# Block 1's first output product: six of its eight units as seven block products each

## The reference

```python
S, D, H = 512, 2048, 8
# first_block: y_mlstm (S, D) and y_sgu (S, D) are both gated activations
x = x + concat([y_mlstm, y_sgu], axis=-1) @ w_out      # w_out (2 D, D), fp32
x = rms_norm(x, final_norm_w)
# second_block: 16 meta tokens are put ahead of x, a layer norm, then two hybrid layers
# (convolution, windowed attention, a gated recurrence), each ending in a product and a layer norm
```

## Time and profile before

| | us |
|---|---|
| median of 3 runs | 3236.39 (3235.48 to 3239.59) |
| the profiled execution's own time | 3235.69 |
| its span, first to last instruction | 3234.2 |
| PE busy | 3149.7 (97%) |
| DVE busy | 2160.9 (67%) |
| ACT busy | 1516.4 (47%) |
| POOL busy | 334.1 (10%) |

### The profile page before, as it was taken

The page is one execution under the profiler, slowest core; times in us unless marked ns, Lnnn a source line. Parts: engine busy times, 40 slices in busy tenths (PEclk is TensorE's granted clock), DMA queues, the critical chain, the costliest instruction groups (busy, mean ns, idle before and its releaser), DMA issues.

```text
span 3234.2 us, 59399 instructions
## 1 busy us (share of the span) xinstructions
PE 3149.7 (97%) x22670; PEld 2932.9 (91%) x22670; DVE 2160.9 (67%) x2930; ACT 1516.4 (47%) x2444; POOL 334.1 (10%) x343
## 2 busy tenths in 40 slices
PE   8999999999999999999979999999997999999998
PEld 7899999999999998788869999999997888888898
DVE  6677888888888888226785655657458565556535
ACT  5345555555555555222254555556226355545521
POOL 1000000000000000000000430440000134314000
PEclk9999999999999999999989999999998999999999
DMA  6344434433434435523334222222333422222522
GB/s 206 92 105 110 107 99 106 124 103 105 110 98 109 108 100 187 182 85 101 102 104 133 67 79 74 60 79 89 137 104 111 138 79 78 72 73 65 171 92 92
DMA packets 449806, 342.51 MB, mean 106 GB/s; under 512 B 20889, under 2 KB 439641, under 8 KB 446449
## 3 DMA queue, kind: packets, MB, share of 16 engines
q1 hardware_dynamic: 431808, 296.28, 31.3%
q0 software_dynamic: 8304, 26.92, 2.3%
q10 hardware_dynamic: 9552, 17.37, 1.6%
HBM read 315.04 MB, written 25.46 MB: 105 GB/s over the span
## 4 chain that ended last, share of the span: by engine, by line
PE 86%; DVE 7%; ACT 3%; DVEq 2%; issue 2%; DMA 1%; ACTq 0%; SPq 0%; POOL 0%
PE ps L696 14%; PE ps L697 14%; PE ps L698 14%; PE ps L866 9%; PE ps L869 9%; PE ps L868 8%; PE ps L1095 2%; PE ps L1256 1%; PE ps L1254 1%; PE ps L1258 1%; PE ps L936 1%; PE ps L702 1%; PE ps L703 1%; PE ps L704 1%; DVE w_low L1947 1%
## 5 line engine op out<-in xcount | busy, mean ns | idle before, releaser
L696 PE MATMUL ps<-x_high,w_high 128*128 128x264 f32 (+3 forms) x3264 | 1068.2, 327 | 52.0 <-DVE w_low L1947 23.0
L697 PE MATMUL ps<-x_low,w_high 128*128 128x264 f32 (+3 forms) x3264 | 1037.6, 318 | 0.0
L698 PE MATMUL ps<-x_high,w_low 128*128 128x264 f32 (+3 forms) x3264 | 1034.9, 317 | 0.0
L696 PEld LDWEIGHTS ps<-x_high,w_high 128*128 128x128 f32 x3264 | 619.1, 190 | 102.9 <-issue 55.8
L1947 DVE TENSOR_TENSOR w_low<-w_raw,w_high 128x1024 fp32r<-128x1024 f32 x332 | 405.6, 1229 | 441.4 <-ACT w_high L1296 416.8
L697 PEld LDWEIGHTS ps<-x_low,w_high 128*128 128x128 f32 x3264 | 619.4, 190 | 44.3 <-issue 3.3
L698 PEld LDWEIGHTS ps<-x_high,w_low 128*128 128x128 f32 x3264 | 617.8, 189 | 41.3
L1296 ACT ACTIVATE w_high<-w_raw 128x1024 fp32r<-128x1024 f32 x332 | 350.2, 1057 | 319.0 <-PE ps L698 247.3
L866 PE MATMUL ps<-x_high,w_high_blocks 128*128 128x256 f32 x1600 | 456.6, 285 | 0.0
L869 PE MATMUL ps<-x_high,w_low_blocks 128*128 128x256 f32 x1600 | 449.4, 281 | 0.0
L868 PE MATMUL ps<-x_low,w_high_blocks 128*128 128x256 f32 x1600 | 449.4, 281 | 0.0
(11 more groups left out here) (471 smaller groups left out, 4817.7 us busy)
## 6 DMA issues: line engine op xcount, KB each, us to landing
w_raw_blocks<-in_w_in SPq DMA_DIRECT2D x200, 512.0 KB, 5.0
w_raw<-in_w_in SPq DMA_DIRECT2D x384, 256.0 KB, 3.2
w_raw<-in_w_out SPq DMA_DIRECT2D x272, 256.0 KB, 3.0
residual<-residual_stream ACTq DMA_DIRECT2D x8, 1056.0 KB, 10.2
residual_stream<-y_layer ACTq DMA_DIRECT2D x2, 2176.0 KB, 9.7
x_natural<-in_x SPq DMA_DIRECT2D x4, 1024.0 KB, 9.3
x_feature_major<-x_stage POOLq DMA_DIRECT2D x4, 1024.0 KB, 6.7
y_sgu_feature_major<-z_silu_g POOLq DMA_DIRECT2D x8, 512.0 KB, 5.1
```

The costliest lines, as they stand in the source:

```text
L696: pe.matmul(dst, wh[:, j, kt, wc], xh[:, k, tok], start=first, stop=False)
L697: pe.matmul(dst, wh[:, j, kt, wc], xl[:, k, tok], start=False, stop=False)
L698: return pe.matmul(dst, wl[:, j, kt, wc], xh[:, k, tok], start=False, stop=last)
```

## The change

Product G keeps two plain units (`PLAIN_G = 2`) and does the other six as block units. What is new around them:

- The four sums of activation blocks are formed by DVE from the staged `y_sgu` (`yst`), before the low weights of the second plain unit, and split by ACT and DVE during that unit; S4's sum is split last, since it goes into the part of x_high and x_low that the second unit still reads.
- The six block units have buffers of their own for the weight sum and the partial results, and use PSUM banks 4 to 6.
- The upper half of `acc` is loaded after three of the sums are split (they lie in its place); the wait for it moves to the fourth block unit (`add_blocks`, k == 8).
- `y_mlstm` is now staged and split around the last block unit, in the manner in which `y_sgu` is before product G.
- PE waits for `c11`, `c12` and `c21` before the meta transposes.
- Loops over product G are written out, and the parameter rows of the second block are loaded later.
- The scratch of POOL's transfers (`dynamic_dma_scratch_size`) is set to 4096 bytes.

```diff
+PLAIN_G = 2
+U_OUT_M = U_OUT_G + PLAIN_G
+SLOT_G = (1, 2, 3, 0, 1, 2, 3)
+def banks_out(e):
+    return tuple(4 + b for b in banks_sgu(e % 3))
...
 # SyncE
-            for d in range(1, 3):
+            for d in range(1, PLAIN_G):
                 load(U_OUT_G + d, cols(w_out, 256 * d, row=KT))
-            sp.wait_ge(x_ready, 2 * KT)
+            for e in range(8 - PLAIN_G):
+                c = 256 * (PLAIN_G + e)
+                load_blocks(S_END + e, c, c + P, 0 if e else PG, w_out, KT)
+            for j in range(4):
+                sp.wait_ge(lo_ready, done(S_GEND - 1, B_S4 if j == 3 else B_S3))
...
             sp.wait_ge(y_st, 32 * H)
             for j in range(4):
+                sp.wait_ge(piece_used, done(S_GEND - 1, B_S2 + j // 2))
                 sp.dma_start(yst[:, 4 * j:4 * j + 4, :], y_md[:, 4 * j:4 * j + 4, :]).then_inc(part_in[j], 16)
 # GpSimd
+            pool.wait_ge(s_low, 14)
             pool.dma_start(acc[:, 8:16, :], x_t[:, 8:16, :]).then_inc(acc_in, 16)
-            pool.wait_ge(y_st, 32 * H)
+            pool.wait_ge(s_low, 16)
             pool.dma_start(mnat[:], a["meta_tokens_2"]).then_inc(meta_in, 16)
...
             pool.wait_ge(acc_in, 48)
+            pool.wait_ge(piece_used, done(S_GEND - 1, B_S3))
             parameters(0)
 # TensorE
-            with pe.Fori(0, 8) as d:
+            for d in range(PLAIN_G):
                 unit(U_OUT_G + d, KT)
-            pe.wait_ge(c21, S_END + 1)
+            pe.wait_ge(ym_done, H + 1)
+            for e in range(8 - PLAIN_G):
+                unit_blocks(S_END + e, banks_out(e), SLOT_G)
+            passed_blocks = NBLOCK_G
+            for n in (c11, c12, c21):
+                pe.wait_ge(n, S_GEND + 1)
 # ScalarE: the last block unit, s + 1 == S_GEND
+                for j in range(3):
                     high(U_OUT_M, j)
+                act.wait_ge(piece_used, done(s, B_S4))
+                for j in range(2):
                     act.wait_ge(part_in[j], 48)
                     fill_piece(j, yst, slice(NM, L))
+                high(U_OUT_M, 3)
+                act.wait_ge(piece_used, done(s, B_A22))
+                act.wait_ge(tmp_used, 2 + 2 * PLAIN_G + 2 * e)
+                corner(s, banks, tmp[:, 0, SH:S])
+                for j in range(2, 4):
+                    act.wait_ge(part_in[j], 48)
+                    fill_piece(j, yst, slice(NM, L))
 # VectorE: ahead of the second plain unit
+            for n, a_, b_, op in ((B_S3, yst[:, K1, T2], yst[:, K1, T1], ALU.subtract), (B_S2, sf_g[B_S3], yst[:, K2, T2], ALU.subtract),
+                                  (B_S1, yst[:, K1, T2], yst[:, K2, T2], ALU.subtract), (B_S4, sf_g[B_S2], yst[:, K2, T1], ALU.add)):
+                dve.drain()
+                if n == B_S4:
+                    dve.wait_ge(y_st, 32 * H)
+                for q in range(2):
+                    ins = dve.tensor_tensor(half(sf_g[n], q), half(a_, q), half(b_, q), op)
+                ins.then_inc(s_sum, 1)
+            dve.wait_ge(acc_in, 32)
...
-    nc = bacc.Bacc("TRN2", target_bir_lowering=False, num_devices=1)
+    nc = bacc.Bacc("TRN2", target_bir_lowering=False, num_devices=1, dynamic_dma_scratch_size=4096)
```

More of the change, by code:

```diff
@@ L71 @@
 U_OUT_G = U_SGU + 3 * PLAIN
-U_OUT_M = U_OUT_G + 8
+PLAIN_G = 2
+U_OUT_M = U_OUT_G + PLAIN_G
 U_LAYER = U_OUT_M + 9
@@ L1613, in norm_mean @@
+            with act.Fori(0, 6) as d:
+                for m in range(2):
+                    act.wait_ge(tmp_used, 16 + 2 * d + m + 1)
+                    take(U_OUT_M + d, m, tmp[:, m, :], ps[:, m, :])
+                    if m == 0:
+                        for j in range(4):
+                            high(U_OUT_M + d + 1, j)
             def norm_mean(n, q):
@@ L2128, in sum_parts, with split_low @@
                 ins.then_inc(s_sum, 1)
-            def split_low(n, src, first):
+            def split_low(n, src, first, blocks=sblk):
                 for q in range(2):
@@ L2491, in _, with add, add_blocks @@
             dve.memset(small[:, 59:60], LN_EPS * EPS).then_inc(tmp_used, 2)
+            def add(U, k):
+                for m in range(2):
+                    dve.wait_ge(evac, 2 * U + m + 1)
+                    dve.tensor_tensor(acc[:, k + m, :], acc[:, k + m, :], tmp[:, m, :], ALU.add).then_inc(tmp_used, 1)
+            def add_blocks(s, k):
+                dve.wait_ge(c21, s + 2)
+                dve.drain()
+                if k == 8:
+                    dve.wait_ge(acc_in, 48)
+                for m in range(2):
+                    dve.tensor_tensor(acc[:, k + m, :], acc[:, k + m, :], tmp[:, m, :], ALU.add).then_inc(tmp_used, 1)
+                dve.drain()
@@ new lines, in _ @@
+            dve.wait_ge(acc_in, 32)
+            for d in range(PLAIN_G):
+                U = U_OUT_G + d
+                if d + 1 < PLAIN_G:
+                    lows(U + 1)
+                    add(U, 2 * d)
+                else:
+                    for i, n in enumerate((B_S3, B_S1, B_S2)):
+                        split_low(n, sf_g[n], 8 + 2 * i, sblk_g)
+                    sum_1(S_END)
+                    sum_3(S_END)
+                    low_block(S_END, B_A11, SLOT_G[B_A11])
+                    sum_2(S_END)
+                    low_block(S_END, B_A12, SLOT_G[B_A12])
+                    low_block(S_END, B_S2, SLOT_G[B_S2])
+                    add(U, 2 * d)
+                    low_block(S_END, B_S1, SLOT_G[B_S1])
+                    sum_4(S_END)
+                    split_low(B_S4, sf_g[B_S4], 14, sblk_g)
@@ new lines, in _ @@
+            for e in range(8 - PLAIN_G):
+                s = S_END + e
+                banks = banks_out(e)
+                low_block(s, B_S3, SLOT_G[B_S3])
+                if e:
+                    add_blocks(s - 1, 2 * PLAIN_G + 2 * e - 2)
+                out_11(s, banks, tmp[:, 0, 0:SH])
+                low_block(s, B_S4, SLOT_G[B_S4])
+                low_block(s, B_A22, SLOT_G[B_A22])
+                if s + 1 < S_GEND:
+                    sum_1(s + 1)
+                    out_22(s, banks, tmp[:, 1, SH:S])
+                    sum_3(s + 1)
+                    low_block(s + 1, B_A11, SLOT_G[B_A11])
+                    sum_2(s + 1)
+                    out_12(s, banks, tmp[:, 1, 0:SH])
+                    low_block(s + 1, B_A12, SLOT_G[B_A12])
+                    low_block(s + 1, B_S2, SLOT_G[B_S2])
+                    low_block(s + 1, B_S1, SLOT_G[B_S1])
+                    sum_4(s + 1)
+                    continue
+                passed_blocks = NBLOCK_G
+                low(U_OUT_M, 0)
+                out_22(s, banks, tmp[:, 1, SH:S])
+                low(U_OUT_M, 1)
+                out_12(s, banks, tmp[:, 1, 0:SH])
+                for j in range(4):
+                    fill_piece(j, yst, slice(NM, L), 2 * KT)
+                    if j == 1:
+                        low(U_OUT_M, 2)
+                        low(U_OUT_M, 3)
+                add_blocks(s, 14)
```

193 lines of the change are left out of this document (112 added, 81 removed).

## The result

The changed kernel takes 3243.38 us (median; 3241.16 to 3247.45), the kernel before in the same comparison 3237.51 us. The ratio is 1.0017, 95% interval 1.0011 to 1.0023: slower by 5.9 us, just inside the 0.2% that the prediction calls no change, and far from its 3226.9 us and above its range. The profiled execution of the changed kernel took 3243.9 us, 8.2 more than the profiled one of before. Every profile here is of one execution; totals are compared as medians, places in time from the profiles.

A forecast was written before the change was run, and what follows sets the result against it. PE, 97% busy, was taken to bound the kernel. Terms -14.0 - 0.6 + 3.6 + 1.5 = -9.5 us gave 3226.9 us from the median 3236.39; forecast range 3224.5 to 3230, eight in ten 3221.8 to 3231.5.

The forecast's parts named there:

- six units: In product G, six block units of 19.91 us replace plain ones of 22.24 us, saving 14.0 us.
- POOL's scratch: At the kernel's start, a smaller descriptor ring could make POOL wait for earlier stores; taken at 0, bounds 0 and 5.
- the end of product G: Before the meta transposes, PE waits for `corner` behind ACT's fills; product M starts 3.6 us later, bounds 2.2 and 6.5.
- The start of product G: At the second plain unit, the wait for acc's upper half goes, eight sums replace it; PE starts 0.6 us earlier.
- the upper bound (6.5): At product G's end, the loss is 6.5 us if a transfer of `y_mlstm` is awaited.
- The clock: At the head of product M, PE runs at half clock after the idle time; 1.5 us lost, bounds 0 and 2.
- the start slips: At kernel start, POOL's stores wait for room, the mask comes late, PE idles up to 5 us; 3227 to 3232, chance 0.07.
- all four rivals: Product G's end costs less (0.22), block units stall (0.12), the start slips (0.07), DVE's chain makes it slower (0.03).
- The rival for the other side: In block units, S3's late low part delays DVE's chain, losing 16.0 us; 3243 us and above, chance 0.03.

The follow-up runs named there:

- 20 more at the start: The changed kernel with 20 more instructions (already met waits) at the start of TensorE's stream; 3230.75 us.
- 20 more ahead of layer 0: The changed kernel with 8192 bytes of scratch, the last block sum copied early, and 20 more TensorE instructions ahead of block 2's layer 0; 3225.75 us.

## Why the prediction was wrong, by its own steps

Its six units saved what it said. It failed because it looked for idle time only where the diff touches the kernel: it had no term for where the loop over head groups lies in TensorE's instruction stream, and that cost 12.9 us. Two more terms were too small, POOL's scratch (1.8 us for 0) and the end of product G (6.05 us for 3.6).

- **Six units, 14.0 us.** Right: 14.3 in the profile, 19.77 us a unit for 19.91, DVE 78% busy for some 80. The chain inside a unit held; the first unit lost 0.4 us in one wait, the others nothing.
- **The start of product G, 0.6 us earlier.** The wait that this step was about did shrink, from 1.73 us to 1.04 ahead of the second plain unit. The profile has 0.8 us lost all the same: PE waited 1.48 and 0.97 us for x_low inside the first unit, where the kernel before waited 0.98 us once. The step took what is ahead of that wait as fixed, and it is not. The stretch from the first matmul of G to the second plain unit took 24.9 to 26.9 us in the eight profiles of the changed kernel and its versions (with 4096 bytes of scratch 25.8 to 26.5, with 8192 bytes 24.9, 25.4 and 26.9), and 25.7 to 27.7 in the four of the kernel before with its own scratch (28.1 with 4096). So a single profile can't tell 0.6 us here, and that the scratch has a part in it is not shown.
- **The end of product G, +3.6 us.** The mechanism was right, the term mis-sized: 6.05 us. The first and third fills waited 0.51 and 0.98 us for `y_mlstm`, what the upper bound (6.5) named, and the transposes ran at half clock (1.86 us instead of 1.16). Taking the last block sum out from behind the fills gave 3.4 us back.
- **The clock, +1.5 us.** Right: 1.9 us. The granted clock was 0.50 (1.2 GHz) in 1454.6 to 1458.5. The counterexample that the prediction set beside it, 1.89 us of idle ahead of product G that slowed nothing, does not hold from run to run: the same 1.89 us is followed by a lower clock in four other runs (20 more at the start, mean 0.83 in 1280 to 1282; the kernel after with 8192 bytes, 0.50; the kernel before with the loop written out, 0.66; 20 more ahead of layer 0, 0.50).
- **POOL's scratch, taken at 0.** Wrong: +1.8 us, inside its bounds of 0 and 5 but not at the 0 that the sum used. The mask was held up by 6.4 us (37.06 to 43.49), where 4.0 of slack were there. The rival "the start slips" had chance 0.07; it should have had more than half, since the edit quartered a resource that four stores of 2048 rows share.
- **What no step named, +12.9 us.** All terms and all four rivals look at places that the diff touches. The instruction stream was not on the list. By itself this is enough for the miss: without the jumps' extra cost the changed kernel takes 3230.75 us, inside the range that the prediction gave eight chances in ten (3221.8 to 3231.5), if not inside its forecast (3224.5 to 3230). The rival for the other side was put at 0.03 and named a mechanism (DVE's chain) that did not occur.

The Trainium skill ("Runtime: NRT & Kernel Launch", Instruction fetch mechanics) states that TensorE's instruction memory holds 2048 instructions, refilled in blocks of 256, and that a taken branch whose target is outside the current window of two such blocks waits for a fetch. The trace agrees with the blocks (1.75 MB in 107 packets) and with the wait. It agrees with neither size: the loop of 1913 instructions would fit into 2048 and is fetched anew in each pass, and the mLSTM loop of 1475, far over two blocks, is not (no piece in 646 to 1297 us of the kernel after). The measurement decides. The section has the cost of crossing a boundary as mostly hidden; right behind a jump it was not, 4 us here. Its advice to write loops out held: 3.3 us for the kernel before, 16.6 for the kernel after.

Open: why a body of 1913 instructions is fetched anew in each pass (9 or 10 pieces a pass) while the mLSTM loop of 1475 and layer 1's loop of 1383 show no such fetching and no idle at their jumps. The limit lies between, and no run here varied it. It is open too what asks for the second piece when it does, 3.4 to 5.5 us behind the first. And that POOL's "issue" waits are waits for room in the scratch was not seen directly, only that they come and go with its size.

## What to carry to other kernels

- Writing out or lengthening code ahead of a long loop moves the loop in the instruction stream. Compare the idle time at every jump back in the profiles of before and after, before you judge the edit: an idle at a loop's first matmul whose named releaser ended long before it was a wait for instructions here, and the queue of instructions shows it. Write the longest loop out, or shift its head by a few instructions.
- An edit that takes memory from a resource (a descriptor ring, a buffer) can have its price at the busiest user of it, however far from the edit. Try the resource alone in the kernel before, and take no more than the edit needs: with 8192 bytes in place of 4096 the 1.8 us at the start shrank to 0.4.
- On an engine that the bottleneck waits for, put the short copy that releases it ahead of the bulk work that nobody waits for yet: 0.36 us of work in the wrong place cost 3.4 us.

## What the runs showed of the hardware that was not expected

- A jump back in the loop of 1913 instructions cost 1.5 to 2.0 us of TensorE's time with 92 or more instructions between the target and the next boundary of 256, and 5.2 to 6.5 us with 3; with 29 there, the wait came in two parts, 1.5 to 1.7 and 1.4 to 2.2 us. The second 16 KB was asked for 3.4 to 5.5 us behind the first.
- After the 5.98 us of idle TensorE ran at half clock, after 1.54 us it did not, so a jump with the long stall costs 6.3 us more than one with the short (12.6 us for two). The stretch from 1870 to 1874 us in the kernel after (19 matmuls; granted clock 0.50 in the third column from the end) and then in the kernel before (30 matmuls; 1.00):

```profile
1870.00:1874.00 4.00, 4.00 (x19) 4.00 (x20) 0.00 (x0) 0.00 (x0) 0.00 (x0) 0.50 0.59 187
```

```profile
1870.00:1874.00 4.00, 4.00 (x30) 3.84 (x29) 2.66 (x3) 1.90 (x3) 0.00 (x0) 1.00 0.78 220
```

- A met wait cost TensorE 0.11 to 0.12 us per instruction of two (21.6 us for 199, 2.37 for 20).
- With 4096 bytes of scratch POOL waited 4.3 to 6.1 us between issues of a 1 MB store, with 8192 bytes 0.7 at most beyond what its semaphores explain.
